# Pads between the HI and LO slots of a split-float32 matmul stream

## What is computed

```python
h = rms_norm(x, norm_mix[layer])
... = jnp.split(h @ w_in[layer], SPLIT_POINTS, axis=-1)
...
x = x + jnp.sum(gate * y, axis=2) @ w_out[layer]
h = rms_norm(x, norm_mlp[layer])
x = x + jnp.square(jax.nn.relu(h @ w_mlp_in[layer])) @ w_mlp_out[layer]
```

## Time and profile before

| | |
|---|---|
| three runs, median | 2828.32 us |
| the profiled execution, span | 2826.7 us |
| TensorE busy (matmul) | 2738.6 us, 97% |
| VectorE busy | 1437.4 us, 51% |
| ScalarE busy | 1165.4 us, 41% |
| DMA moved | 672.57 MB, mean 238 GB/s |

### The profile page before, as it was taken

How to read it: one execution, slowest core, us unless ns; L and a number is a source line. 1 busy time by engine, 2 the same in 40 slices (tenths; PEclk the granted TensorE clock), 3 DMA queues, 4 the chain that set the end, 5 groups by cost and what they waited for, 6 DMA issues and landing times.

```text
span 2826.7 us, 33251 instructions
## 1 busy us (share of the span) xinstructions
PE 2738.6 (97%) x12784; PEld 2077.6 (73%) x12784; DVE 1437.4 (51%) x1645; ACT 1165.4 (41%) x1520; POOL 12.9 (0%) x20
## 2 busy tenths in 40 slices
PE   8999899999999999999999999999999999989896
PEld 6888677778888888888888788888888785434332
DVE  4444355656655565555556744577654463212122
ACT  4444355654354444444444644455444441000001
POOL 0000000000000000000000000000000000000000
PEclk9999999999999999999999999999999999999999
DMA  8765845557556555555555476555555459999997
GB/s 287 288 216 209 295 159 172 174 198 246 211 184 227 189 193 185 187 192 192 186 187 180 170 279 210 192 190 171 207 192 186 161 180 371 427 427 426 427 427 321
DMA packets 115680, 672.57 MB, mean 238 GB/s; under 512 B 12126, under 2 KB 17678, under 8 KB 40689
## 3 DMA queue, kind: packets, MB, share of 16 engines
q1 hardware_dynamic: 86048, 612.52, 59.1%
q10 hardware_dynamic: 27264, 46.58, 4.6%
q0 software_dynamic: 2256, 11.95, 1.2%
HBM read 647.37 MB, written 28.35 MB: 239 GB/s over the span
## 4 chain that ended last, share of the span: by engine, by line
PE 85%; DMA 6%; DVE 4%; ACT 3%; issue 1%; DVEq 1%; ACTq 0%; SPq 0%
PE PS L315 23%; PE PS L317 23%; PE PS L316 22%; PE PS L2114 8%; DMA WIDE<-in_w_down 3%; DMA WIDE<-in_w_up 2%; DVE LO L273 1%; PE PS L339 1%; PE PS L2012 1%; ACT HI L271 1%; PE PS L2280 1%; DMA WIDE<-in_w_gate 1%; PE PS L1468 1%; PE PS L929 0%; PE PS L1621 0%
## 5 line engine op out<-in xcount | busy, mean ns | idle before, releaser
L273 DVE TENSOR_TENSOR LO<-RAW,HI 128x1024 fp32r<-128x1024 f32 x760 | 922.8, 1224 | 838.2 <-ACT HI L271 834.2
L315 PE MATMUL PS<-HI,XH 128*128 128x512 f32 x3040 | 1207.4, 397 | 23.8 <-DVE LO L273 15.7
L317 PE MATMUL PS<-HI,XL 128*128 128x512 f32 x3040 | 1186.5, 390 | 0.0
L316 PE MATMUL PS<-LO,XH 128*128 128x512 f32 x3040 | 1185.6, 390 | 0.0
L271 ACT ACTIVATE HI<-RAW 128x1024 fp32r<-128x1024 f32 x760 | 793.6, 1057 | 778.6 <-PE PS L317 682.8
L315 PEld LDWEIGHTS PS<-HI,XH 128*128 128x128 f32 x3040 | 572.3, 188 | 149.2 <-DVE LO L273 20.9
L317 PEld LDWEIGHTS PS<-HI,XL 128*128 128x128 f32 x3040 | 572.0, 188 | 121.0
L316 PEld LDWEIGHTS PS<-LO,XH 128*128 128x128 f32 x3040 | 572.7, 188 | 117.8 <-issue 2.9
L2114 PE MATMUL PS<-WIDE,XS 128*64 128x512 f32 x1024 | 229.4, 596 | 24.1 <-DMA WIDE<-in_w_up 15.8
L2114 PEld LDWEIGHTS PS<-WIDE,XS 128*64 128x64 f32 x1024 | 75.3, 137 | 162.5 <-issue 162.0
L2114 PE MATMUL PS<-WIDE,Y 128*64 128x512 f32 x496 | 113.0, 598 | 7.8 <-ACT Y L2169 5.5
(11 more groups left out here) (400 smaller groups left out, 1353.7 us busy)
## 6 DMA issues: line engine op xcount, KB each, us to landing
RAW<-in_w_in SPq DMA_DIRECT2D x132, 1024.0 KB, 4.9
RAW<-in_w_mlp_in SPq DMA_DIRECT2D x64, 1024.0 KB, 4.8
RAW<-in_w_mlp_out SPq DMA_DIRECT2D x64, 1024.0 KB, 4.8
WIDE<-in_w_gate SPq DMA_DIRECT2D x64, 1024.0 KB, 23.2
WIDE<-in_w_up SPq DMA_DIRECT2D x64, 1024.0 KB, 19.2
WIDE<-in_w_down SPq DMA_DIRECT2D x64, 1024.0 KB, 21.9
RAW<-in_w_out SPq DMA_DIRECT2D x32, 1024.0 KB, 4.8
RAW<-in_xattn_wkv SPq DMA_DIRECT2D x32, 1024.0 KB, 4.9
```

The costliest lines, as they stand in the source:

```text
L273: dve.tensor_tensor(r["lo"][:, hl, :], r["raw"](k), r["hi"][:, hl, :].bitcast(F32), ALU.subtract).then_inc(lo_done, 1)
L315: pe.matmul(o, xh, wh, start=kt == 0, stop=False)
L316: pe.matmul(o, xh, wl, start=False, stop=False)
L317: mm = pe.matmul(o, xl, wh, start=False, stop=kt == kn - 1)
```

## The change

A slot of HI becomes 8 floats longer (4128 bytes) and a slot of LO 28 floats longer (4208 bytes); ScalarE, VectorE and TensorE use the first 1024 of each as before. HI still begins at 154624, so its slots begin at 0, 32, 64 and 96 modulo 512. LO begins at 171136, and its slots at 128, 240, 352 and 464. A pad of 96 floats stands behind LO, and WORK begins at 188352, which is 448 modulo 512. FINAL must lie where WORK begins, so a pad of 240 floats (960 bytes) stands ahead of it; XS and ROUNDED move by the same 960 bytes, to 448 modulo 512. XH, XL, RAW, Y, WIDE and all ahead of HI stay where they are. The instructions and their order are the same on every engine.

```diff
         RAW = work_memory.enter_context(nc.sbuf_tensor("RAW", [P, RAW_SLOTS, BLK], F32))
-        HI = work_memory.enter_context(nc.sbuf_tensor("HI", [P, HL_SLOTS, BLK], F32R))
-        LO = work_memory.enter_context(nc.sbuf_tensor("LO", [P, HL_SLOTS, BLK], F32R))
+        HI = work_memory.enter_context(nc.sbuf_tensor("HI", [P, HL_SLOTS, BLK + 8], F32R))
+        LO = work_memory.enter_context(nc.sbuf_tensor("LO", [P, HL_SLOTS, BLK + 28], F32R))
+        work_memory.enter_context(nc.sbuf_tensor("shift_work", [P, 96], F32))
         WORK = work_memory.enter_context(nc.sbuf_tensor("WORK", [P, 10240], F32))
...
-            act.activation(r["hi"][:, hl, :], r["raw"](k), ACT.Copy).then_inc(hi_done, 1)
+            act.activation(r["hi"][:, hl, 0:BLK], r["raw"](k), ACT.Copy).then_inc(hi_done, 1)
             dve.wait_ge(hi_done, it * per + (splits(b) + 1))
-            dve.tensor_tensor(r["lo"][:, hl, :], r["raw"](k), r["hi"][:, hl, :].bitcast(F32), ALU.subtract).then_inc(lo_done, 1)
+            dve.tensor_tensor(r["lo"][:, hl, 0:BLK], r["raw"](k), r["hi"][:, hl, 0:BLK].bitcast(F32), ALU.subtract).then_inc(lo_done, 1)
...
+        sb("shift_final", [P, 240])
         sb("FINAL", [P, 2048])
```

## The result

The changed kernel takes 2866.38 us (2864.04 to 2867.76) against 2828.04 us measured beside it: a ratio of 1.0136, with a 95% interval of 1.0124 to 1.0148. That is 38 us slower. The forecast was 2805 us, and the measured time also lies 4 us above the upper end of the range.

What follows compares the result with a forecast made beforehand. TensorE's matmul pace was taken to bound the first stage, DMA the last. 2.5 ns x 9120 = 23 us less, other terms 0, gave 2804 us of span, 2805 us unprofiled; range 2764 to 2862 us.

Steps and rivals of the forecast that it cites:

- The bound: First stage set by TensorE's own matmul pace, last stage by DMA; time won or lost before 2340 us moves the end one for one.
- That the pace depends on addresses: First-stage matmuls lose 13.4 ns each, 122 us in all, when 4-byte columns are read beside weight loads; gating rows suggested addresses matter.
- So remainder 0 is not a good one in this sample: Gating product, lines 695 to 697: loss 10.0 ns with weights at remainder 0, others as much as 29% better.
- best stretch: Eight gating-product intervals around k = 3 to 5, 113.8 ns each, a loss of 7.1 ns.
- the ratio 9.1 to 10.0: Gating product's average loss against remainder 0, applied to the big product's 13.4 ns: 1.2 ns less, 11 us; middle taken, 2.5 ns.
- ScalarE and VectorE at 0: Work on padded HI and LO slots, 1057 and 1224 ns, stays covered by TensorE's 2720 ns block: counted 0.
- WORK and its neighbours at 0: WORK, FINAL, XS and ROUNDED beginning at 448 modulo 512: counted 0, with 3 us to either side.
- DMA at 0: RAW and WIDE keep their addresses, loads still fit a faster TensorE, and the last stage keeps its 430 us.
- Rival 1: First-stage stream: the steady pace is favourable, pads force restarts in 760 blocks; 12 to 43 us slower, middle 2856 us; chance 0.37.
- Rival 2: First-stage stream: weights cover all 512 bytes whatever the start, so 226.7 ns stays and time is 2828 us; chance 0.20.
- Rival 3: First-stage stream: reads no longer meet, loss falls towards 1.5 ns; up to 109 us less, 2719 us; chance 0.05.
- The signs named beforehand: TensorE starts within a block: mean near 224 ns for the forecast, rigid 226.7 for no change, 231 and 236 for restarts.

Runs made afterwards that it cites:

- The stream alone: Kernels running only TensorE's three-matmul form, without the reference's work or other engines beside it; start remainders varied, settled at 226.7 ns a matmul at distance 0.

## Why the prediction was wrong

- **The bound** was read correctly. TensorE's own pace sets the first stage, the last one waits for DMA and kept 426 GB/s, and 38.9 us lost in the first came out as 37.2 us of span.
- **That the pace depends on addresses** was right. So was the place, the float32r stream at the full clock. Float32 doesn't show it. The float32 matmuls of the earlier trace rows have their moving operand in WORK and the stationary one in Y, at 0. WORK is at 0 modulo 512 in the kernel before, at 448 in the one with only WORK and its neighbours moved, and at 64 in the one with HI and LO at 64. Four rows take 1.02 us in each of the three, and start 215 ns apart; here the second and the third:

```profile
1752.93 1.02 PE L1293 MATMUL PS<-WORK,Y 128*128 128x256 f32 x4
```
```profile
1766.00 1.02 PE L1293 MATMUL PS<-WORK,Y 128*128 128x256 f32 x4
```

- **Two rows were read less carefully, without effect on the forecast.** The four rows are two matmuls of line 1292: a float32 matmul stands in the trace as two records, so it costs four cycles per column, not two, and the surplus is 1.7 ns a record. And in the stretch of the earlier trace rows the window view shows no halved clock; it was inferred from the pace. A later stretch settles it, with a granted clock of 0.50 and again 427 ns from start to start:

```profile
295.10:298.30 3.20, 3.20 (x8) 2.52 (x9) 0.89 (x1) 0.00 (x0) 0.00 (x0) 0.50 0.97 381
```

- **The step that failed is "So remainder 0 is not a good one in this sample".** It compared three intervals of the gating product at remainder 0 (116.7 ns) with eight at other remainders (113.8 ns). The three were the first behind another stream, and so most likely show a start, not the cost of remainder 0. The stream alone, with 256 moving and 64 stationary columns at distance 0, starts with 116, 117 and 117 ns too and then settles at 113.3 ns, the value of the "best stretch" (24 columns were not run). The rows with 24 stationary columns could also not stand for 128: at 512 moving columns and distance 0 a narrower stationary operand is slower. The next step, the ratio 9.1 to 10.0 carried over to 13.4 ns, rested on that alone. Its -2.5 ns should have been +4.8 ns.
- **The other terms of the sum** held: ScalarE and VectorE at 0 (1059 and 1224 ns), WORK and its neighbours at 0 (ratio 1.000), DMA at 0.
- **Rival 1** had the sign, and its upper end was near the size (43 us against 38). Its own argument, that the settled pace was a favourable one, was the better reading of the same trace: the 231 ns behind a restart are also near what the stream takes with mixed distances. It was right, too, that the loop settles into one of several phases: at 240 bytes the same addresses run at 233.3 or 236.7 ns, by what came before. But it charged a restart to each block and took the middle, 28 us. The runs show that a constant distance is dear by itself, with no restart in it, so it is paid on all twelve intervals and the sum lies near the upper end.
- **Rival 2** fell. The Trainium skill's SBUF — State Buffer, section "Who interferes with whom", calls TensorE's two read ports independent, and this stream does not agree: with nothing changed but the start of one operand against the other, its pace went from 226.7 to 236.7 ns. That section's other statement, that TensorE never waits for another engine, is not touched, as no other engine was at work. The runs don't show which part of TensorE or its memory waits.
- **Rival 3** fell: of the 148 float32r settings with 512 moving columns, none settled below 226.7 ns.
- **The signs named beforehand** told the cases apart. Intervals like 231 and 236 ns in every block were to show rival 1, and they are there; the mean near 224 ns is not, and a rising mean was named as the sign of an error in sign.

## What to carry to other kernels

Where float32r matmuls of 512 columns follow each other, let the moving and the stationary operand begin at the same remainder modulo 256, and let that remainder be a multiple of 32 (0, 32, 64 and 128 were tried; 16 and 48 cost 1.5%). A constant offset of a multiple of 16 bytes costs 1 to 4.4% of the stream, and mixed offsets cost about 2%. One short run of a setting is not its only possible pace, as the same addresses can settle in two ways. A pad that moves everything moves the DMA destinations as well, so look at the stage that is full of transfers too. And when short rows from a trace are to stand for a steady state, first ask whether the engine had settled in them; a stretch right behind another kind of work has not.

## What the runs showed of the hardware that I had not expected

- The pace of a float32r stream goes with the distance between the moving and the stationary start, and repeats to 0.05 ns after 256 bytes: 226.7 ns at 0, 228.9 to 236.7 ns at the other multiples of 16. Distance 0 is cheap only with both starts at a multiple of 32 bytes; at 16 or 48 it takes 230.0 ns.
- Some settings have two steady paces, and what ran before picks one: 233.3 and 236.7 ns at 240 bytes in one kernel, 231.1 and 233.3 ns with HI at 0 and LO at 128 in one stream.
- With HI and LO at one distance of a multiple of 16 bytes from the stationary operand at 0, the stream settles into a pattern of at most seven intervals that repeats to within 1 ns, such as 234 and 239 ns in turn at 240 bytes, or 226, 229 and 232 ns at 64. At distance 0 it is a constant 226.7 ns after two to nine intervals.
- At distance 0 the surplus over one column per cycle is 32 cycles with 256, 320, 384 or 512 columns. Why it is 32, and why fewer stationary columns raise it at 512 moving columns (230.0 ns with 64) and lower it at 256 (113.3 against 120.0 ns), stays open. At a granted clock of 0.50 (1.2 GHz) there is no surplus: 512 columns take 427 ns, which is 512 cycles.
- Moving all buffers by 32 or 64 bytes lowered the DMA rate of a full stage from 427 to 420 or 421 GB/s; moving them by 256 bytes did not.
